# A transformer block's first stage on one Trainium2 core: its order of work rewritten, and four small products spread over the array

## The chip, the core and the metric

The kernel runs on one core of one Trainium2 chip. The metric is the device time of one execution in microseconds (us), and the number given for a kernel is the median of its runs. The core's engines are named as in the profile: PE is TensorE's matrix work and PEld its weight loads, DVE is VectorE, ACT is ScalarE, POOL is GpSimd, and SP is the queue on which most transfers are issued. PSUM is the memory that PE writes, in eight banks of 128 x 512 floats, which the code calls ps[0] to ps[7].

## The reference, cut to what matters

Two transformer blocks are computed for 256 tokens of width 1024. Only the beginning of the first concerns the change: the conditioning vectors c and c_ctx give a shift and a scale for the tokens x and for the context ctx; both are normalised and modulated with them; the results, called hT (tokens) and hcT (context) when turned so that features lie on the partitions, are multiplied by w_in. Beside it, filters for a long convolution come out of a small network with two sines, and their spectrum out of a Fourier matrix.

```python
x = x + _pos_embed_2d(ROWS)
mod_x = split(silu(c) @ w_ada[l] + b_ada[l], 6); mod_c = split(silu(c_ctx) @ w_ada[l] + b_ada[l], 6)
def project(h, mod):
    p = _modulate(_rmsnorm(h, norm_mix_g[l]), mod[0], mod[1]) @ w_in[l]
    q, k, v, g, a_f, a_b, hy = split(p, PROJ_SPLITS)
    la_f = log_sigmoid(a_f @ gla_wa_f[l] + gla_ba_f[l]) / 16      # la_b in the same way
hdn = sin(freq * (z @ w1 + b1)); hdn = sin(freq * (hdn @ w2 + b2))
h = (hdn @ w3).reshape(L, 2, 2, 512) * exp(-t * deltas)           # the filters
```

After this come gated linear attention, the long convolution, a mixture of experts, and a second pair of attention and feed-forward layers. The change leaves these as they are.

## The kernel before

Each engine runs its own list of instructions, written out by hand in one order; counters (semaphores) let one engine wait for another. There is no scheduler: an instruction that waits holds up all that stand behind it on its engine. Weights come in tiles of 128 rows through a ring of 12 slots, in the order of `load_order`; a slot is loaded again when `tiles_done`, which PE raises, says that its last user is through.

The first stage ends where the products for q, k and v begin (L1849 to L1851, three products of split operands each). On PE the functions of this stage are:

- `ada(m, k0, k1)` (L1787): conditioning row m = 0 (shift) or 1 (scale), 128 x 32 weights in four column groups at once, four weight tiles at a time.
- `mod(i, m)` (L1796): turns a finished row into columns, eight products of two columns. ACT copies the row out of PSUM before (`row`, L761) and the columns after it (`mod`, L767); four small POOL operations (L665 to L668) then make the factors a_mix and b_mix.
- `turn(src, ready)` (L1775): turns the normalised tokens xn or the context cn, 16 transposes; ACT copies the result to hT or hcT (`taken`, L754).
- `taps(o)` (L1812): four products of the filter network's last layer, for filter order o. DVE makes the filters of it (`filters`, L1207 to L1210).
- `spectrum(o)` (L1821 to L1823): ten products with the Fourier matrix. ACT copies the five results to spec (L775 to L779) and raises `ft_taken`.
- the loop over k = 0 to 7 that follows: per tile of w_in two wide products for the gate g (L1870, 512 columns each, weights hT) and two narrow ones (L1873, 32 x 256), of hT and of hcT, for the input of the decay gates. Before the change, `spectrum(1)` stands in the middle of this loop.

The products for q, k and v wait for `ft_taken` 2, since they write the banks that spectrum(1) used, and for `lo_ready` 1: the first tile of w_in must have been split in two parts, by ACT (`split_in`, L816) and then DVE (`low_in`, L1245). On ACT, `split_in(0)` stands behind the five copies of spectrum(1). This stretch of ACT's list is the same before and after the change:

```python
act.copy(hT_parts[0], hT[:, :, :]).then_inc(hcT_ready, 1)
act.wait_ge(hcT_ready, KD)
act.copy(hcT_parts[0], hcT).then_inc(hcT_ready, 1)
spectrum(1)
...
for i in range(PARTS_1):
    split_in(i)
```

Behind the products for q, k and v, four products with only 33 rows (L1901) give the decay gates' arguments; ACT and DVE take their logarithm, which the cumulative sums need after the first eight tiles of the hyena products (the next L1849 to L1851).

## Time and profile before

| | us |
|---|---|
| runs of the kernel before | 1566.29, 1573.41, 1570.35; median 1570.35 |
| the profiled execution | 1564.88, of which the span from its first to its last instruction is 1563.0 |
| PE busy in the span | 1317.6 (84%) |
| DVE, ACT busy | 639.7, 498.4 |
| first product for q, k and v starts at | 92.47 |

All places in the trace are microseconds from the start of the span of this one execution, and durations too are those of this execution. It took 5.47 us less than the median of the runs. Records of fp32 products come in pairs, so that eight records of L1812 are four products; a record's duration includes its way through the array, and back to back they follow each other sooner than they last.

### The profile page before, as it was taken

The page shows a single profiled execution, that of the slowest core. Times are in us where ns is not written, and L with a number is a line of the kernel's source. Part 1 is how long each engine was busy: PE and PEld are TensorE (multiplying, and loading weights), DVE is VectorE, ACT ScalarE, POOL GpSimd, SP SyncE. Part 2 cuts the span into 40 slices and gives each one's busy share as a digit, 9 for nine tenths or more (in the row PEclk, how much of TensorE's full clock was granted, in tenths as well). Part 3 has the DMA queues.
Part 4 walks back from the last instruction along what each step waited for, and adds up shares of the span by engine and source line. Part 5 has one row for each costly group of instructions (what it writes and reads, how often), then busy time and mean ns, then how long its engine had stood idle before and what let it go on. Part 6 is the DMA issues. An engine that isn't in the chain of part 4 may idle for free.

```text
span 1563.0 us, 22568 instructions
## 1 busy us (share of the span) xinstructions
PE 1317.6 (84%) x9346; PEld 968.9 (62%) x9346; DVE 639.7 (41%) x913; ACT 498.4 (32%) x757; POOL 103.1 (7%) x115
## 2 busy tenths in 40 slices
PE   5999899976655565655689999999999999999998
PEld 1468665731111111101186999999999987999997
DVE  4324545430100100100187575556545447565654
ACT  2423532320000000000157544345343437444443
POOL 0000011000000000000017000000000007000000
PEclk9999999888886967887799999999999999999999
DMA  9433536969999999999952356655666751355562
GB/s 354 156 108 83 161 135 242 413 275 416 420 419 419 420 419 419 420 419 419 384 186 63 109 174 196 189 167 162 194 190 184 205 171 55 97 165 172 178 205 74
DMA packets 136870, 376.55 MB, mean 241 GB/s; under 512 B 8392, under 2 KB 55929, under 8 KB 136608
## 3 DMA queue, kind: packets, MB, share of 16 engines
q1 hardware_dynamic: 134952, 373.81, 66.1%
q10 hardware_dynamic: 1848, 1.74, 0.3%
q8 instruction: 52, 0.85, 0.2%
q14 instruction: 18, 0.15, 0.0%
HBM read 373.42 MB, written 1.05 MB: 240 GB/s over the span
## 4 chain that ended last, share of the span: by engine, by line
PE 62%; DMA 20%; DVE 9%; ACT 4%; SPq 3%; issue 1%; POOL 1%; DVEq 0%; ACTq 0%
PE psum L1849 14%; PE psum L1851 14%; PE psum L1850 14%; DMA ring<-in_w_up 6%; DMA ring<-in_w_down 6%; DMA work<-in_w_gate 5%; PE psum L2139 4%; SPq L542 3%; DMA tokens<-in_w_down 1%; DVE parts L1496 1%; DVE route L1527 1%; POOL work L719 1%; PE psum L1870 1%; PE psum L2236 1%; PE psum L2011 1%
## 5 line engine op out<-in xcount | busy, mean ns | idle before, releaser
L1849 PE MATMUL psum<-parts 128*128 128x256 f32 (+1 forms) x1672 | 496.0, 297 | 12.9 <-DVE parts L1502 9.2
L1850 PE MATMUL psum<-parts 128*128 128x256 f32 (+1 forms) x1672 | 493.7, 295 | 0.0
L1851 PE MATMUL psum<-parts 128*128 128x256 f32 (+1 forms) x1672 | 493.4, 295 | 0.0
L1496 DVE TENSOR_TENSOR parts<-ring,parts 128x1024 fp32r<-128x1024 f32 x232 | 280.8, 1227 | 168.4 <-ACT parts L988 167.7
L1849 PEld LDWEIGHTS psum<-parts 128*128 128x128 f32 x1672 | 321.0, 192 | 24.4 <-issue 13.5
L1850 PEld LDWEIGHTS psum<-parts 128*128 128x128 f32 x1672 | 321.1, 192 | 7.3 <-issue 0.2
L1851 PEld LDWEIGHTS psum<-parts 128*128 128x128 f32 x1672 | 321.0, 192 | 7.3
L988 ACT CAST parts<-ring 128x1024 fp32r<-128x1024 f32 x232 | 239.8, 1045 | 248.2 <-PE psum L1851 211.5
L2139 PE MATMUL psum<-ring,work 128*32 128x512 f32 x512 | 87.8, 823 | 64.8 <-DMA ring<-in_w_up 34.3
L978 ACT ACTIVATE work<-psum 128x1024 f32<-128x1024 f32 x4 | 4.1, 1023 | 381.9 <-PE psum L2139 381.9
L2139 PE MATMUL psum<-work 128*32 128x512 f32 x512 | 83.8, 796 | 48.5 <-DMA work<-in_w_gate 29.3
L1479 DVE TENSOR_TENSOR work<-work,psum 128x1024 f32<-128x1024 f32 x4 | 4.9, 1220 | 271.1 <-ACT work L978 271.1
L2139 PEld LDWEIGHTS psum<-ring,work 128*32 128x32 f32 x512 | 16.6, 132 | 136.8 <-DMA ring<-in_w_up 52.5
L719 POOL TENSOR_SCALAR work<-work 128x256 f32<-128x256 f32 (+1 forms) x64 | 71.0, 1112 | 436.0 <-DVE work L1592 432.7
L2139 PE MATMUL psum<-early,work 128*32 128x512 f32 x384 | 56.6, 722 | 37.5 <-DMA early<-in_w_down 20.1
L2139 PEld LDWEIGHTS psum<-work 128*32 128x32 f32 x512 | 16.9, 130 | 111.3 <-DMA work<-in_w_gate 44.6
L1484 DVE SCALAR_TENSOR_TENSOR work<-psum,work,gate_ffn 128x512 f32<-128x512 f32 x8 | 5.6, 746 | 148.9 <-PE psum L2139 148.9
L2139 PEld LDWEIGHTS psum<-early,work 128*32 128x32 f32 x384 | 11.6, 121 | 79.7 <-DMA early<-in_w_down 29.8
L1079 ACT ACTIVATE work<-tokens 128x512 f32<-128x512 f32 x22 | 13.9, 632 | 104.0 <-DVE tokens L1626 104.0
L1849 PE MATMUL psum<-work_parts,ring_parts 128*128 128x256 f32 x144 | 42.3, 294 | 2.5 <-DVE ring_parts L1245 2.4
L1245 DVE TENSOR_TENSOR ring_parts<-ring,ring_parts 128x1024 fp32r<-128x1024 f32 (+1 forms) x24 | 25.0, 1046 | 47.1 <-ACT ring_parts L816 47.0
L1048 ACT ACTIVATE work<-work 128x257 f32<-128x257 f32 (+1 forms) x64 | 35.5, 557 | 23.6 <-DVE work L1592 23.5
(341 smaller groups left out, 1444.5 us busy)
## 6 DMA issues: line engine op xcount, KB each, us to landing
ring<-in_w_qkv_b SPq DMA_DIRECT2D x72, 512.0 KB, 4.3
work<-in_w_gate SPq DMA_DIRECT2D x16, 2048.0 KB, 23.0
ring<-in_w_up SPq DMA_DIRECT2D x16, 2048.0 KB, 23.4
ring<-in_w_ada SPq DMA_DIRECT2D x48, 512.0 KB, 8.2
work<-in_w_down SPq DMA_DIRECT2D x12, 2048.0 KB, 23.1
ring<-in_w_gate SPq DMA_DIRECT2D x44, 512.0 KB, 4.0
ring<-in_w_up SPq DMA_DIRECT2D x44, 512.0 KB, 5.4
ring<-in_w_down SPq DMA_DIRECT2D x44, 512.0 KB, 4.3
```

What stands on the lines that cost most here:

```text
L542: sp.dma_start(out, d[name][0, bass.ds(expert, EG), P * k:P * k + P, :].rearrange("j p n -> p j n")).then_inc(full, 16)
L719: ins = pool.tensor_scalar(bias_d[:, n % 2, j, 0:SPAN[layer]], dist[:, p], SLOPE[2 * k + j], None, ALU.mult)
L988: act.copy(part_of(hi_slots, t, n), ring[:, slot_2(t), 0:n]).then_inc(hi_ready, 1)
L1048: ins = act.activation(row, row, ACT.Exp, scale=-1.0, bias=nmax[:, p, h:h + 1], accum_out=den[:, p, h:h + 1])
L1245: dve.tensor_tensor(lower, w, high, ALU.subtract).then_inc(lo_ready, 1)
L1496: dve.tensor_tensor(part_of(lo_slots, t, n), ring[:, slot_2(t), 0:n], part_of(hi_slots, t, n), ALU.subtract).then_inc(lo_ready, 1)
L1527: return dve.tensor_reduce(sq_sum[:, L * i:L * i + L], sq.rearrange("p k l -> p l k"), AX.X, ALU.add)
L1849: pe.matmul(out, lhsT[0], rhs[0], start=start, stop=False, skip_group_check=True)
L1850: pe.matmul(out, lhsT[0], rhs[1], start=False, stop=False, skip_group_check=True)
L1851: return pe.matmul(out, lhsT[1], rhs[0], start=False, stop=stop, skip_group_check=True)
L1870: pe.matmul(ps[5 + t], hT[:, k, P * t:P * t + P], w[:, 0:V_W], start=(k == 0), stop=(k == KD - 1))
L2139: ins = pe.matmul(ps[bank + n][rows, :], lhsT[:, k, rows], w[:, j, 512 * n:512 * n + 512], start=(k == 0), stop=(k == KD - 1))
```

## The change

The conditioning products move between the parts of the filter network, the tokens are normalised and turned earlier and the context later, and the context is turned into the same banks 0 to 3 that the tokens used. The gate products wait for hT tile by tile (`hT_ready` counts to 8 for its eight parts, so later counts rise by 7 or 1). The narrow products leave the loop, follow the eight pairs of wide ones, and write partitions 0 to 31 and 64 to 95 of bank 7, in two column groups. The gates' input and its weights wa are laid out twice, at partitions 0 and 64, and the four products alternate between the two groups of rows. spectrum(1) comes last. The diff, cut to its core (the rest renumbers counters and lays out wa and aT for 97 partitions, which makes the transfer of wa 97 x 512 floats in place of 33 x 512, and splits DVE's copy to aT in two of 32 x 256):

```diff
-            sp.dma_start(decay, d["c_decay"].rearrange("p (a t h) -> p a t h", a=2, t=TT)).then_inc(filter_loaded, 16)
             sp.dma_start(consts[:, :], d["c_ident"]).then_inc(x_loaded, 16)
-            sp.dma_start(cn, d["ctx"][0].rearrange("(t p) d -> p t d", p=P)).then_inc(ctx_loaded, 16)
-            sp.dma_start(dft, d["c_dft"].rearrange("p (t f) -> p t f", t=TT)).then_inc(filter_loaded, 16)
             for t in load_order:
                 src, n = stream[t]
+                if t == upto_tile["ada0"]:
+                    sp.dma_start(decay, d["c_decay"].rearrange("p (a t h) -> p a t h", a=2, t=TT)).then_inc(filter_loaded, 16)
+                    sp.dma_start(dft, d["c_dft"].rearrange("p (t f) -> p t f", t=TT)).then_inc(filter_loaded, 16)
+                if t == upto_tile["ada1"]:
+                    sp.dma_start(cn, d["ctx"][0].rearrange("(t p) d -> p t d", p=P)).then_inc(ctx_loaded, 16)
...
-            for i in range(2):
+            def sine(i):
                 act.wait_ge(sin_arg, i + 1)
                 act.activation(hid[:, 2], hid[:, 0], ACT.Sin).then_inc(sin_done, 1)
 
+            def token_norm(i, x, out):
+                for t in range(TT):
+                    ins = act.activation(out[:, t], x[:, t], ACT.Square, accum_out=stats[:, 2 * i + t:2 * i + t + 1])
+                ins.then_inc(squared, 1)
+
+            def token_root(i):
+                act.wait_ge(ms_ready, i + 1)
+                act.activation(stats[:, 8 + 2 * i:10 + 2 * i], stats[:, 4 + 2 * i:6 + 2 * i], ACT.Sqrt).then_inc(std_ready, 1)
+
+            sine(0)
             act.wait_ge(x_placed, 1)
-            for t in range(TT):
-                act.activation(xn[:, t], xres[:, t], ACT.Square, accum_out=stats[:, t:t + 1])
-            act.wait_ge(ctx_loaded, 16)
-            for t in range(TT):
-                ins = act.activation(sq[:, t], cn[:, t], ACT.Square, accum_out=stats[:, 2 + t:3 + t])
-            ins.then_inc(squared, 1)
-            act.wait_ge(ms_ready, 1)
-            act.activation(stats[:, 8:12], stats[:, 4:8], ACT.Sqrt).then_inc(std_ready, 1)
+            token_norm(0, xres, xn)
+            sine(1)
+            token_root(0)
...
+            taken(1, hT)
             row(0)
+            mod(0)
             spectrum(0)
-            mod(0)
             row(1)
-            taken(1, hT)
             mod(1)
+            act.wait_ge(ctx_loaded, 16)
+            token_norm(1, cn, sq)
+            token_root(1)
...
+                if i == 0:
+                    dve.wait_ge(x_loaded, 48)
+                    dve.tensor_tensor(xres[:, :, :], xres[:, :, :], pos, ALU.add).then_inc(x_placed, 1)
+
+            def token_norm(i, x, out):
+                dve.wait_ge(squared, i + 1)
+                dve.tensor_scalar(stats[:, 4 + 2 * i:6 + 2 * i], stats[:, 2 * i:2 * i + 2], 1.0 / D, EPS, ALU.mult, ALU.add).then_inc(ms_ready, 1)
+                dve.wait_ge(std_ready, i + 1)
+                link(dve.reciprocal(stats[:, 12 + 2 * i:14 + 2 * i], stats[:, 8 + 2 * i:10 + 2 * i]))
+                for t in range(TT):
+                    at = 12 + 2 * i + t
+                    ins = dve.tensor_scalar(out[:, t], x[:, t], stats[:, at:at + 1], None, ALU.mult)
+                ins.then_inc(xn_ready, 1)
+
+            token_norm(0, xres, xn)
...
+                dve.tensor_scalar(hT[:, k, :], hT[:, k, :], a_mix[:, k, 0:1], b_mix[:, k, 0:1], ALU.mult, ALU.add).then_inc(hT_ready, 1)
+            token_norm(1, cn, cn)
...
+            ada(0, 0, 4)
+            pe.wait_ge(xn_ready, 1)
+            turn(xn, xt_ready)
+            ada(0, 4, 8)
+            pe.wait_ge(xt_taken, 1)
             taps(0)
-            ada(0, 0, 4)
+            mod(0, 0)
+            ada(1, 0, 4)
             pe.wait_ge(filter_loaded, 32)
             spectrum(0)
-            ada(0, 4, 8)
-            ada(1, 0, 8)
-            mod(0, 0)
-            pe.wait_ge(xn_ready, 1)
-            pe.wait_ge(ft_taken, 1)
-            turn(xn, xt_ready)
+            ada(1, 4, 8)
             mod(1, 1)
-            pe.wait_ge(xn_ready, 2)
-            pe.wait_ge(mod_taken, 2)
-            turn(cn, xt_ready, 4)
-            pe.wait_ge(xt_taken, 1)
-            taps(1)
 
             def products(out, lhsT, rhs, start, stop):
                 pe.matmul(out, lhsT[0], rhs[0], start=start, stop=False, skip_group_check=True)
                 return w_parts[i % PARTS_1]
 
 
-            pe.wait_ge(hT_ready, 1)
-            pe.wait_ge(xt_taken, 2)
+            ws = []
             for k in range(KD):
-                if k == 4:
-                    spectrum(1)
-                w = tile()
+                ws.append(tile())
+                pe.wait_ge(hT_ready, k + 1)
                 for t in range(TT):
-                    pe.matmul(ps[5 + t], hT[:, k, P * t:P * t + P], w[:, 0:V_W], start=(k == 0), stop=(k == KD - 1))
+                    pe.matmul(ps[5 + t], hT[:, k, P * t:P * t + P], ws[k][:, 0:V_W], start=(k == 0), stop=(k == KD - 1))
+                if k == 3:
+                    pe.wait_ge(xn_ready, 2)
+                    pe.wait_ge(ft_taken, 1)
+                    turn(cn, xt_ready)
+                if k == 5:
+                    pe.wait_ge(xt_taken, 2)
+                    taps(1)
+            for k, w in enumerate(ws):
                 pe.wait_ge(hcT_ready, k + 1)
                 for s, h in enumerate((hT, hcT)):
-                    ins = pe.matmul(ps[7][0:2 * RANK, L * s:L * s + L], w[:, V_W:V_W + 2 * RANK], h[:, k, :],
-                                    start=(k == 0 and s == 0), stop=(k == KD - 1), skip_group_check=True)
+                    ins = pe.matmul(ps[7][HID * s:HID * s + 2 * RANK, 0:L], w[:, V_W:V_W + 2 * RANK], h[:, k, :],
+                                    start=(k == 0), stop=(k == KD - 1), skip_group_check=True)
                 ins.then_inc(tiles_done, 1)
+            spectrum(1)
...
-            for i, b in enumerate((7, 0, 1, 2)):
+            for i, (b, s, t) in enumerate(((7, 0, 0), (1, 1, 0), (0, 0, 1), (2, 1, 1))):
                 if i == 1:
                     pe.wait_ge(q_taken, 1)
-                pe.matmul(ps[b], aT[:, P * i:P * i + P], wa, start=True, stop=True).then_inc(gatein_ready, 1)
+                rows = slice(HID * s, HID * s + 2 * RANK + 1)
+                pe.matmul(ps[b], aT[rows, P * t:P * t + P], wa[rows], start=True, stop=True).then_inc(gatein_ready, 1)
 
```

PE's list in the opening, with what each first instruction waits for. Before the change (L1812 taps, L1787 ada, L1821 spectrum, L1796 mod, L1775 turn, L1870 the first gate product; "ring_full" counts a weight tile's landing, and the rows left out are the further products of the same call):

```order
L1812 MATMUL psum<-work 128x512 [waits sin_done]
...
L1787 MATMUL psum<-ring,gate_ffn 32x512 [waits ring_full2,ring_full1,ring_full3,ring_full0,cond_ready]
...
L1821 MATMUL psum<-work,early 128x512 [waits filt_ready,filter_loaded]
...
L1787 MATMUL psum<-ring,gate_ffn 32x512 [waits ring_full6,ring_full7,ring_full5,ring_full4]
...
L1787 MATMUL psum<-ring,gate_ffn 32x512 [waits ring_full10,ring_full9,ring_full11,ring_full8,row_taken]
...
L1787 MATMUL psum<-ring,gate_ffn 32x512 [waits ring_full2,ring_full3,ring_full1,ring_full0]
...
L1796 MATMUL psum<-consts,early 128x2 [waits row_taken]
...
L1775 MATMUL psum<-consts,tokens 128x128 [waits ft_taken,xn_ready]
...
L1796 MATMUL psum<-consts,early 128x2 [waits mod_taken,row_taken]
...
L1775 MATMUL psum<-consts,work 128x128 [waits mod_taken,xn_ready]
...
L1812 MATMUL psum<-work 128x512 [waits xt_taken]
...
L1870 MATMUL psum<-ring,tokens 128x512 [waits ring_full4,xt_taken,hT_ready]
```

After it, in the lines of the changed kernel (L1801 ada, L1789 turn, L1826 taps, L1810 mod, L1835 spectrum, L1878 the gate products):

```order
L1801 MATMUL psum<-ring,gate_ffn 32x512 [waits ring_full1,ring_full2,ring_full0,ring_full3,cond_ready,sin_done]
...
L1789 MATMUL psum<-consts,tokens 128x128 [waits xn_ready]
...
L1801 MATMUL psum<-ring,gate_ffn 32x512 [waits ring_full6,ring_full7,ring_full5,ring_full4]
...
L1826 MATMUL psum<-work 128x512 [waits xt_taken]
...
L1810 MATMUL psum<-consts,early 128x2 [waits row_taken]
...
L1801 MATMUL psum<-ring,gate_ffn 32x512 [waits ring_full10,ring_full9,ring_full11,ring_full8,row_taken]
...
L1835 MATMUL psum<-work,early 128x512 [waits filt_ready,filter_loaded]
...
L1801 MATMUL psum<-ring,gate_ffn 32x512 [waits ring_full2,ring_full3,ring_full1,ring_full0]
...
L1810 MATMUL psum<-consts,early 128x2 [waits mod_taken,row_taken]
...
L1878 MATMUL psum<-ring,tokens 128x512 [waits hT_ready,ring_full4]
```

The first ada and the turning of xn stand ahead of the taps, and the second mod stands directly ahead of the gate products; the turning of cn and the second taps have left the opening.

PE's list at the end of the stage, before the change (L1870 wide, L1873 narrow, L1849 the first product for q, k and v):

```order
L1873 MATMUL psum<-tokens,ring 32x256 [waits hcT_ready]
...
L1870 MATMUL psum<-ring,tokens 128x512 [waits ring_full10]
...
L1873 MATMUL psum<-tokens,ring 32x256 [waits hcT_ready]
L1873 MATMUL psum<-work,ring 32x256
L1870 MATMUL psum<-ring,tokens 128x512 [waits ring_full11]
L1870 MATMUL psum<-ring,tokens 128x512
L1873 MATMUL psum<-tokens,ring 32x256 [waits hcT_ready]
L1873 MATMUL psum<-work,ring 32x256
L1849 MATMUL psum<-work_parts,ring_parts 128x256 [waits lo_ready,hT_ready,ft_taken]
```

and after it (L1878 wide, L1889 narrow, L1835 to L1837 the second spectrum, L1859 the first product for q, k and v):

```order
L1878 MATMUL psum<-ring,tokens 128x512 [waits hT_ready,ring_full10]
...
L1878 MATMUL psum<-ring,tokens 128x512 [waits hT_ready,ring_full11]
...
L1889 MATMUL psum<-tokens,ring 32x256 [waits hcT_ready]
L1889 MATMUL psum<-work,ring 32x256
...
L1889 MATMUL psum<-tokens,ring 32x256 [waits hcT_ready]
L1889 MATMUL psum<-work,ring 32x256
L1835 MATMUL psum<-work,early 128x512 [waits filt_ready]
...
L1836 MATMUL psum<-work,early 128x512
L1837 MATMUL psum<-work,early 1x512
L1859 MATMUL psum<-work_parts,ring_parts 128x256 [waits lo_ready,hT_ready,ft_taken]
```

The spectrum stood ten products of the gate loop ahead of the q, k and v products' wait for `ft_taken` and `lo_ready`; now it stands immediately ahead of it.

SP's list of transfers after the change, in its first part (L530 is the identity, L540 weight tiles, L534 and L535 the decay and Fourier tables, L537 the context):

```order
L530 DMA consts<-in_c_ident 128x130
L540 DMA ring<-in_w_ada 128x1024 x8
L534 DMA work<-in_c_decay 128x2048
L535 DMA early<-in_c_dft 128x1024
L540 DMA ring<-in_w_ada 128x1024 x4
L540 DMA ring<-in_w_ada 128x1024 [waits tiles_done] x4
L537 DMA work<-in_ctx 128x2x1024
L540 DMA ring<-in_w_in 128x544 [waits tiles_done] x8
```

Before, decay, context and Fourier tables, 2.5 MB together, were issued ahead of the first weight tile.

## Rows read from the trace of the kernel before

**Rows 1.** The page, the chain that ended last, by engine.
```profile
PE 62%; DMA 20%; DVE 9%; ACT 4%; SPq 3%; issue 1%; POOL 1%; DVEq 0%; ACTq 0%
```

**Rows 2.** Timeline of PE, opening: start us, us, work, idle before.
```profile
17.19 7.19 PE L1812 MATMUL psum<-work 64*128 64x512 f32 x8 [3.39 <-ACT work L738]
24.43 3.64 PE L1787 MATMUL psum<-ring,gate_ffn 128*32 128x512 f32 x16
29.49 2.05 PE L1821 MATMUL psum<-work,early 128*128 128x512 f32 x2 [1.42 <-DVE work L1210]
...
43.11 3.64 PE L1787 MATMUL psum<-ring,gate_ffn 128*32 128x512 f32 x32 [1.15 <-ACT early L761]
46.68 1.95 PE L1796 MATMUL psum<-consts,early 128*128 128x2 f32 x16
48.49 1.95 PE L1775 MATMUL psum<-consts,tokens 128*128 128x128 f32 x16
...
52.62 3.21 PE L1775 MATMUL psum<-consts,work 128*128 128x128 f32 x16 [0.50 <-ACT early L767]
55.76 4.05 PE L1812 MATMUL psum<-work 64*128 64x512 f32 x8
```

**Rows 3.** Timeline of PE, the gate products to the first split product.
```profile
60.18 1.95 PE L1870 MATMUL psum<-ring,tokens 128*128 128x512 f32 x4 [0.37 <-issue]
...
63.05 1.98 PE L1870 MATMUL psum<-ring,tokens 128*128 128x512 f32 x4
...
71.73 1.13 PE L1821 MATMUL psum<-work,early 128*128 128x512 f32 x2
...
92.47 0.39 PE L1849 MATMUL psum<-work_parts,ring_parts 128*128 128x256 f32 x1
```

**Rows 4.** Chain that ended last, one piece inside the second spectrum.
```profile
74.58 0.86 PE psum L1822 x2
```

**Rows 5.** Timeline of DVE, the same stretches.
```profile
16.61 2.28 DVE L1198 TENSOR_TENSOR xres<-xres,work 128x2048 f32<-128x2048 f32 x1
...
29.91 1.42 DVE L1218 TENSOR_SCALAR tokens<-xres,stats 128x1024 f32<-128x1024 f32 x2
...
53.74 2.67 DVE L1228 TENSOR_SCALAR tokens<-tokens,a_mix,b_mix 128x256 f32<-128x256 f32 x8 [21.09 <-POOL b_mix L668]
...
85.04 2.36 DVE L1245 TENSOR_TENSOR ring_parts<-ring,ring_parts 128x1024 fp32r<-128x1024 f32 x2 [14.51 <-ACT ring_parts L816]
```

**Rows 6.** Timeline of ACT, the same stretches.
```profile
23.20 1.28 ACT L748 ACT_TABLE_LOAD   x1
...
50.47 1.93 ACT L754 COPY tokens<-psum 128x1024 f32<-128x1024 f32 x2 [0.72 <-PE psum L1775]
...
81.00 0.58 ACT L775 COPY early<-psum 128x512 f32<-128x512 f32 x1 [13.19 <-PE psum L1823]
...
83.97 1.99 ACT L816 CAST ring_parts<-ring 128x1024 fp32r<-128x1024 f32 x2
```

**Rows 7.** Timeline of SP, the issue of the position table.
```profile
3.86 0.47 SPq L529 DMA_DIRECT2D work<-in_c_pos  x1
```

**Rows 8.** DMA issues up to 100 us: KB each, us to landing.
```profile
work<-in_c_pos SPq DMA_DIRECT2D x1, 1024.0 KB, 9.0
```

**Rows 9.** Windows; last three columns: granted clock, DMA share, GB/s.
```profile
15.00:20.00 5.00, 2.81 (x4) 1.25 (x5) 3.75 (x6) 1.50 (x4) 0.00 (x0) 1.00 1.03 420
50.00:55.00 5.00, 4.50 (x34) 4.44 (x33) 1.26 (x4) 2.00 (x3) 0.91 (x4) 0.81 0.99 374
130.00:140.00 10.00, 8.57 (x23) 4.21 (x22) 7.66 (x8) 4.07 (x6) 3.51 (x1) 0.75 0.19 58
140.00:150.00 10.00, 10.00 (x79) 10.00 (x79) 6.19 (x9) 6.80 (x5) 0.00 (x0) 0.91 0.22 54
```

**Rows 10.** Timeline of PE around the gate input and hyena products.
```profile
133.71 4.23 PE L1901 MATMUL psum<-early 33*128 33x512 f32 x6 [0.60 <-ACT early L828]
...
138.77 0.55 PE L1849 MATMUL psum<-work_parts,ring_parts 128*128 128x256 f32 x1 [0.83 <-DVE ring_parts L1245]
```

69 lines of the change are left out of this document (29 added, 40 removed).

## The prediction

> **What bounds the kernel now.** I read the page first. PE holds 62% of the chain that ended last and transfers 20% [rows 1], but the mean says little about the first stage, so I went to the timelines of its engines. From the first taps at 17.19 to the first product for q, k and v at 92.47, PE is the engine in front: the list below has waits of only 1.42, 1.15, 0.50 and 0.37 us [rows 2, 3]. The stage takes 75.3 us, and its end starts a long dense run of products. So what counts is the time at which that first product starts, and whatever delays it should delay the rest: the stages behind it wait for their predecessors' results, the expert weights' transfers too.
>
> Two more things are to be seen. The first taps take 7.19 us and the second, the same eight records, 4.05; 32 records of ada take 3.64 us at 43.11 and 16 take as long at 24.43 [rows 2]. So PE runs at its lower level, 1.2 GHz, from the start until the first spectrum. It falls there again near 53 us: the granted clock of 50 to 55 is 0.81 [rows 9], and the second turning takes 3.21 us where the first took 1.95 [rows 2]. Before that fall PE had two-column products, transposes and a wait.
>
> **The opening, step by step, on the changed order.** Adding the position table (2.28 us, [rows 5]) now stands between the two sines. The table lands at 3.86 + 9.0 = 12.9 [rows 7, 8], the identity, issued next, about 0.2 later (estimate from its 65 KB at 420 GB/s, [rows 9]), so the sum ends at 15.4. The second sine's chain took the 3.39 us of idle time before the taps [rows 2]; now it ends at 18.8, 1.6 later than before. The first four weight tiles landed by 24.43, since ada found them there [rows 2]. With 2.5 MB fewer ahead of them, at 420 GB/s, they land by 18.4 at the latest: no wait. The tiles of the second half, 2.1 MB behind, come by 23.4.
>
> - ada(0), first half: 18.8 to 22.4, the 3.64 us of the lower level.
> - The root for xn: table load 1.28 and scaling 1.42 [rows 5, 6], and some 0.4 of small operations (estimate), so xn is there at 21.9, under that ada.
> - Turning xn takes 1.95 us at the upper and 3.21 at the lower level [rows 2]. I take 2.3, to 24.7. ACT copies it in 1.93 [rows 6], to 26.6; ada's second half (half of 3.64, so 1.8) fits beneath.
> - taps 4.05, to 30.7. DVE's filters follow: taps ended at 24.38 before and the spectrum began at 29.49, 5.1 us [rows 2], so the spectrum can begin at 35.8. mod (1.81, from 46.68 to 48.49) and ada(1), first half (1.8), end at 34.4 beneath it, unless the clock falls again; I allow 0.7 for that.
> - spectrum: 71.73 to the copy at 81.00, 9.3 us [rows 3, 6], to 45.8.
> - ACT must now copy the spectrum (81.00 to 83.97, 3.0 us [rows 6]) before row(1), whose copy is the 1.15 us that PE waited at 43.11 [rows 2]. ada(1)'s second half hides under that, the rest is a new wait of 2.3 us. mod(1) then runs from 49.9 to 51.7, or 52.2 with 0.5 for a lower clock.
> - From the end of mod(1) to the first gate product lie ACT's copy, POOL's four operations and one of DVE's eight: PE's mod ended at 50.27 + 1.84 = 52.1, DVE began at 53.74 [rows 5], and its first eighth takes 0.3. That is 2.0 us, under which the old order had turned cn. It is now open. Gate products start at 54.2, against 60.18 [rows 3].
>
> **The gate products and the end.** Two records of full products take 0.86 us [rows 4], so a tile's four wide records take 1.72. A tile took 63.05 - 60.18 = 2.87 with its narrow ones [rows 3]: 1.72, 0.86 for the narrow four at half the width, and 0.3 for going to and fro between the shapes. After the change: eight times 1.72 is 13.8; the turning of cn is 1.9 and the second taps 4.3 with their switch, both taken from the opening. The context's normalisation, eight hT parts (2.67, [rows 5]) and the copies beside them have 6.9 us of wide products before they are wanted, and the second filters (5.1) have two wide pairs and the narrow products (7.2). So these cost nothing; if any came 1 us late, PE would wait that 1 us.
>
> The narrow products in two column groups: no row has two groups. Ada has four, with a record every 3.64 / 32 = 0.114 us [rows 2], so 32 narrow records would take 3.6, against 6.9 one after another. I take 3.6 plus 0.2. From 54.2: 13.8 + 1.9 + 4.3 + 3.8 brings 78.0. PE has stood in small products and waits from 47.6 to 54.2, so I expect the clock to fall, as it did near 53. At the other place where PE stood and had small products, from 132 on, the windows 130 to 150 lose 0.25 x 10 + 0.09 x 10 = 3.4 us of clock [rows 9], of which about half fell on working PE; the fall near 53 cost 1.3. I take 2.1, bounds 1.3 and 3.4: 80.1. The spectrum brings 89.4.
>
> Here is the change's price. Before, the copies of spectrum(1), and the split of the first tile behind them on ACT and DVE, ran under four tiles of gate products. Now nothing lies between. From 81.00 through the splitting casts at 83.97 and DVE's first half of 2.36, begun at 85.04 [rows 5, 6], is 5.2 us, all of it open: 94.6. The clock falls during it, 1.9 more: 96.5. Against 92.47 that is **+4.0 us**.
>
> **The gate input** in two row groups. It occupied PE from 133.71 to 137.94, but the hyena products began at 138.77, released by DVE's split of their first tile [rows 10]. Its saving, at most half of 4.23, is thus hidden; if DVE were faster by over 0.8, it would show. I count zero, and -2.1 as the bound. DVE's copy to aT in two pieces and the longer transfer of wa lie under q, k and v: zero, at most 0.3.
>
> Own time: 1564.88 + 4.0 = 1568.9. The median of the runs was 5.47 above that execution, so the predicted median is 1570.35 + 4.0, rounded 1574.5 us.
>
> **The rivals.** *The clock stays low through the opening.* In the trace PE was at work for 7.19 and then 3.64 us and stayed at 1.2 GHz [rows 2]. If the same holds with ada and the turning in front, then turning ends at 25.6, ada at 29.3, the taps' 7.2 at 36.5, mod and ada (double) at 43.8, the spectrum, partly low, at 54.8. That is 9 later than 45.8: +13, 1583, slower by over 0.5%. It decides as soon as the lower level lasts to about 35 us. Against it: at 53 to 57 a turning of 3.21 was followed by quick taps, so a dense stretch of transposes did bring the clock back. The Trainium skill (TensorE: Matmul & The Clock Gate, part 1) has the clock rise with sustained activity; by it the old taps should have raised it, and they did not, while the new mix would raise it and give the sum above. I give this rival 0.14.
>
> *Column groups do not overlap.* Then 3.3 us are added: +7.3, 1577.7. For it: no row has two groups at partitions 0 and 64. Against it: ada's four overlap fully. The Trainium skill (TensorEngine Tiling, Key Properties) says that tiles load and multiply in parallel, which would be the 3.6. Chance 0.07.
>
> *The delay is given back or the gains are larger.* The opening delivers gate products 6 us earlier, and if the wait at the end cost nothing, because ACT's copies or the split ran beneath something, the sum would be 4.0 - 5.2 - 1.9 = -3: 1567. Together with the gate input's 2.1 it is 1565; past 0.5% it comes only with another few us that I cannot place. Against it: ACT's list keeps the split behind the copies. Chance 0.19, of which 0.06 lies below 1562.5.
>
> **How the numbers follow.** My forecast, 0.60, has its own range: with every clock loss at its lower bound and turning at 1.95 the sum is +1, with all at the upper and ada's second half low it is +8: 1571 to 1578.5. The range for 8 in 10 reaches to both sides, from the small gain to near the low clock's case: 1566 to 1582. About 0.5%, 7.9 us, is what a measurement here can tell from no change. Slower by more: the low clock's 0.14, half of the column groups', 0.05 of the forecast: 0.22. Faster by more: 0.06, rounded 0.07. Within: 0.71.
>
> **What would show it.** Right: gate products begin near 54; narrow records come every 0.11; PE idles some 5 us after the second spectrum, with a granted clock below 1 there; the first q, k, v product starts at 94 to 98; the gate input shortens and hyena products still wait for DVE. Wrong: taps of 7 us again; an idle time at the end under 2 us; q, k, v below 91; or a difference of more than 2 us that arises behind the hyena products.

## The result and the profile after

| | before | after |
|---|---|---|
| median of 20 runs each, us | 1568.27 (1560.51 to 1574.57) | 1574.24 (1571.37 to 1577.34) |
| ratio after to before | | 1.0041, 95% interval 1.0029 to 1.0053 |
| profiled execution, us (span) | 1564.88 (1563.0) | 1576.28 (1574.4) |

The changed kernel is slower by 0.41%, 6.4 us (4.5 to 8.3). That is clear of no difference at all, and for the most part inside the 0.5% that the prediction took as no change. The forecast was +4.0 on the median that was shown, 1574.5; the kernel before came 2.1 us lower in these runs, so the forecast of the time is met to 0.3 us and that of the difference missed by 2.4. The closeness of the first is luck. The two profiled executions differ by 11.4 us, because that of before lies 3.4 us below its median and that of after 2.0 above: not the spans are to be compared but places inside them.

First PE's timeline of the changed kernel, from the first product of ada to the first product of q, k, v (start us, us, work, idle time before in brackets with its releaser); it answers to [rows 2, 3].

```profile
18.63 3.64 PE L1801 MATMUL psum<-ring,gate_ffn 128*32 128x512 f32 x16 [4.73 <-ACT work L740]
25.24 1.92 PE L1801 MATMUL psum<-ring,gate_ffn 128*32 128x512 f32 x16
27.32 3.70 PE L1826 MATMUL psum<-work 64*128 64x512 f32 x8 [0.16 <-ACT tokens L760]
36.14 1.10 PE L1835 MATMUL psum<-work,early 128*128 128x512 f32 x2 [1.39 <-DVE work L1233]
49.39 1.95 PE L1810 MATMUL psum<-consts,early 128*128 128x2 f32 x16 [2.34 <-ACT early L767]
53.37 9.76 PE L1878 MATMUL psum<-ring,tokens 128*128 128x512 f32 x16 [2.03 <-DVE tokens L1240]
62.97 1.91 PE L1789 MATMUL psum<-consts,work 128*128 128x128 f32 x16
64.71 3.60 PE L1878 MATMUL psum<-ring,tokens 128*128 128x512 f32 x8
69.91 4.80 PE L1826 MATMUL psum<-work 64*128 64x512 f32 x8 [1.60 <-ACT work L760]
74.64 5.95 PE L1878 MATMUL psum<-ring,tokens 128*128 128x512 f32 x8
80.52 0.40 PE L1889 MATMUL psum<-tokens,ring 128*32 128x256 f32 x1
80.76 0.38 PE L1889 MATMUL psum<-tokens,ring 128*32 128x256 f32 x1
84.10 1.12 PE L1835 MATMUL psum<-work,early 128*128 128x512 f32 x2
98.77 0.55 PE L1859 MATMUL psum<-work_parts,ring_parts 128*128 128x256 f32 x1 [5.45 <-DVE ring_parts L1257]
```

Gate products begin at 53.37, 6.8 us sooner than at 60.18 [rows 3]; the first product of q, k, v begins at 98.77, 6.3 later than at 92.47. So the stretch between these two rows has grown by 13 us. Some 5.4 of them are no loss: the context's turning (1.74 to the next row) and the second taps (3.6 at the upper level) stood in the opening before. And the narrow products in column groups save about as much again. The waits and the slow stretches thus cost some 13 us. Four things are to be seen in the list: a wait of 5.45 at the end, as forecast; one of 1.60 ahead of the second taps, which was not; and two stretches in which the same records take longer: 16 wide ones 9.76 and eight 5.95, where eight take 3.60 between them. The taps between them are slower too, 4.80.

The windows of the changed kernel say why (granted clock, DMA share and GB/s are the last three columns):

```profile
50.00:55.00 5.00, 2.97 (x14) 2.09 (x15) 2.19 (x7) 2.25 (x5) 0.91 (x4) 0.69 0.80 329
55.00:60.00 5.00, 5.00 (x9) 2.01 (x8) 2.15 (x6) 0.20 (x1) 0.00 (x0) 0.63 0.46 154
70.00:75.00 5.00, 5.00 (x9) 1.83 (x10) 0.19 (x1) 4.25 (x9) 0.00 (x0) 0.74 0.03 6
95.00:100.00 5.00, 1.23 (x6) 1.26 (x7) 2.60 (x3) 4.97 (x7) 0.00 (x0) 0.63 0.00 2
```

Each fall to the lower level stands behind small products or a wait: mod and its waits ahead of 53, the 1.60 ahead of 70, the 5.45 ahead of 99. The third has to be read with care. The prediction put its price ahead of the first product of q, k, v, but the loss lies behind the row 98.77. From the first product for q, k, v to the first hyena product it took 46.30 us before and takes 48.25 now, 1.95 more. The products for q, k and v are the same, and what the gate input behind them saved on PE was waited for again (below). So the start of the hyena products is the better place at which to compare the two kernels. PE's timeline there, in the changed kernel, answers to [rows 10]:

```profile
141.96 1.98 PE L1919 MATMUL psum<-early 33*128 33x512 f32 x6 [0.60 <-ACT early L837]
147.02 0.55 PE L1859 MATMUL psum<-work_parts,ring_parts 128*128 128x256 f32 x1 [3.08 <-DVE ring_parts L1257]
```

147.02 - 138.77 = +8.25 us, as much as the whole loss by the ratio and more. Behind this place the two profiled executions differ by another 3.15 us (11.4 in all); against the kernel before, the other kernels' traces differ there by between -2.4 and +2.8, so I read nothing into it. The gate input's six records shrank from 4.23 to 1.98, and PE's wait for DVE in front of the hyena products grew from 0.83 to 3.08 by the same 2.25: no gain.

Not all of the 2.25 is the row groups' doing. The run e6 below has this part as it was, four products on one group of rows, and there (PE's timeline, and a window):

```profile
130.08 2.84 PE L1903 MATMUL psum<-early 33*128 33x512 f32 x6 [0.60 <-ACT early L828]
130.00:133.00 3.00, 2.84 (x6) 1.04 (x6) 3.00 (x3) 0.57 (x3) 3.00 (x1) 1.00 0.38 152
```

The granted clock is 1.00 there, and was 0.79 from 133.7 to 136 and 0.50 from 136 to 138 in the kernel before. So 0.86 us are the row groups' (2.84 to 1.98, both at the upper level), and 1.39 the place of the clock's fall.

The wait of 1.60 has its cause on ACT. Its timeline (ACTq is its instruction queue, which issues DMAs):

```profile
57.10 0.31 ACTq L800 DMA_DIRECT2D early<-in_wa  x1
59.83 7.58 ACTq L804 DMA_DIRECT2D route<-in_c_iota  x1
67.93 1.93 ACT L760 COPY work<-psum 128x1024 f32<-128x1024 f32 x2 [12.13 <-issue]
93.36 0.58 ACT L781 COPY early<-psum 128x512 f32<-128x512 f32 x1 [14.92 <-PE psum L1837]
96.33 1.99 ACT L825 CAST ring_parts<-ring 128x1024 fp32r<-128x1024 f32 x2
```

The turned context was in PSUM by 64.9, but ACT copied it at 67.93 because an issue held its list for 7.58 us. In the kernel before, the same issue:

```profile
55.46 2.17 ACTq L795 DMA_DIRECT2D route<-in_c_iota  x1
```

Until about 63 other transfers share the engines, and from then to the end of the issue nearly nothing else moves. Three windows of the changed kernel, and then its group of wa in the view of DMA issues (KB each):

```profile
60.00:62.00 2.00, 2.00 (x6) 0.91 (x5) 0.00 (x0) 0.00 (x0) 0.00 (x0) 1.00 0.99 341
64.00:66.00 2.00, 2.00 (x12) 1.29 (x10) 0.00 (x0) 0.00 (x0) 0.00 (x0) 1.00 0.07 26
66.00:68.00 2.00, 2.00 (x6) 0.76 (x4) 0.00 (x0) 0.07 (x1) 0.00 (x0) 1.00 0.07 26
```

```profile
early<-in_wa ACTq DMA_DIRECT2D x1, 194.0 KB
```

A DMA share of 0.07 is one of the 16 engines (0.0625), and the issue ended at 67.41, when that lone traffic did: the share of 66 to 67.4 is 0.06 and that of 67.4 to 69 is 0.41. My reading was that wa, whose 33 rows became 97, goes through a single engine, and that an issue behind it waits until this has drained. 194 KB at 26 GB/s take 7.6 us, like the stall, but the transfer was issued at 57.10, 10.3 us before the stall's end, and other traffic was on the engines for much of that, so that this match proves nothing. What exactly the issue waits for (room in a queue, I supposed) no run shows.

### The profile page after: what moved, and what is told of

Read it like the earlier page. It is cut to its first block, busy times and chain, and to the rows that moved or that the text cites. A ratio compares the mean times of both kernels' runs of the same rounds, so it can differ in the third digit from the quotient of the medians.

```text
span 1574.4 us, 22580 instructions
## 1 busy us (share of the span) xinstructions
PE 1317.1 (84%) x9346; PEld 975.3 (62%) x9346; DVE 640.2 (41%) x917; ACT 499.0 (32%) x758; POOL 103.2 (7%) x115
## 4 chain that ended last, share of the span: by engine, by line
PE 61%; DMA 18%; DVE 9%; ACT 5%; SPq 4%; issue 1%; POOL 1%; ACTq 1%; DVEq 0%
PE psum L1859 14%; PE psum L1860 14%; PE psum L1861 14%; DMA ring<-in_w_up 6%; DMA ring<-in_w_down 6%; DMA work<-in_w_gate 5%; PE psum L2157 5%; SPq L544 4%; DVE parts L1510 1%; DVE route L1541 1%; PE psum L2029 1%; PE psum L2254 1%; POOL work L721 1%; PE psum L2022 1%; PE psum L2277 1%
## 5 line engine op out<-in xcount | busy, mean ns | idle before, releaser
L1859 PE MATMUL psum<-parts 128*128 128x256 f32 (+1 forms) x1672 | 496.7, 297 | 12.9 <-DVE parts L1516 9.2
L1859 PEld LDWEIGHTS psum<-parts 128*128 128x128 f32 x1672 | 321.7, 192 | 24.4 <-issue 13.8
L2157 PE MATMUL psum<-ring,work 128*32 128x512 f32 x512 | 82.3, 777 | 72.0 <-DMA ring<-in_w_up 36.3
L2157 PE MATMUL psum<-work 128*32 128x512 f32 x512 | 86.0, 815 | 42.8 <-DMA work<-in_w_gate 24.6
L1859 PE MATMUL psum<-work_parts,ring_parts 128*128 128x256 f32 x144 | 43.2, 300 | 10.2 <-DVE ring_parts L1257 10.1
```

The source lines that it names most:

```text
L1859: pe.matmul(out, lhsT[0], rhs[0], start=start, stop=False, skip_group_check=True)
L2157: ins = pe.matmul(ps[bank + n][rows, :], lhsT[:, k, rows], w[:, j, 512 * n:512 * n + 512], start=(k == 0), stop=(k == KD - 1))
```

## The experiments

The theory: the loss has three parts, the open wait behind the second spectrum with its clock loss, the stall of wa with the clock loss that follows from it, and the loss in the opening, against gains from the column groups. The rivals are named run by run. All edits are to the changed kernel, except that of e6. "Hyena" is the start of the hyena products against 138.77 in the kernel before.

| kernel | executions | ratio to before | 95% | in us | q, k, v at | hyena |
|---|---|---|---|---|---|---|
| the change | 20 | 1.0041 | 1.0029 to 1.0053 | +6.4 | 98.77 | +8.3 |
| e1 spectrum ahead of narrow | 10 | 1.0010 | 0.9988 to 1.0032 | +1.6 | 93.91 | +3.0 |
| e2 split ahead of copies | 10 | 1.0010 | 0.9988 to 1.0031 | +1.6 | 95.93 | +6.2 |
| e3 issues late | 8 | 1.0034 | 1.0017 to 1.0052 | +5.3 | 98.97 | +8.7 |
| e4 wait filled | 10 | 1.0023 | 1.0010 to 1.0036 | +3.6 | 97.83 | +6.9 |
| e5 wa on 128 rows | 10 | 1.0018 | 1.0004 to 1.0033 | +2.8 | 93.21 | +2.8 |
| e6 columns only | 7 | 0.9967 | 0.9946 to 0.9989 | -5.2 | 88.79 | -3.6 |
| e7 row first | 4 | 1.0059 | 1.0038 to 1.0079 | +9.2 | 100.40 | +9.4 |
| e8 combined | 10 | 0.9969 | 0.9954 to 0.9984 | -4.9 | 87.50 | -5.0 |
| e9 wa on 98 rows | 1 | | | | 94.04 | +4.2 |
| e10 wa on 106 rows | 1 | | | | 92.54 | +2.7 |

The last column comes from one trace each, and the ratios' intervals are some 4 to 7 us wide; still the two agree within 5 us everywhere, and within 1 in three of the nine that have both. The intervals of e1 to e5 and e7 overlap that of the change, some only at the edge. So for the single edits the mechanism is read from the traces, and only e6 and e8 are told from the change by their times alone. A trace's places scatter too: from the first q, k, v product to the first hyena product the six traces with the same end wait of 5.45 took 47.8 to 48.9 us.

**e1, the second spectrum ahead of the narrow products.**

```diff
+            spectrum(1)
             for k, w in enumerate(ws):
                 pe.wait_ge(hcT_ready, k + 1)
...
-            spectrum(1)
```

> The changed kernel with its second spectrum put ahead of the eight narrow pairs instead of behind them. Theory (the exposed end chain: after the spectrum come ACT's copies, 3.0 us, and the split of the first tile, 2.4 us, with PE idle for 5.45): the narrow products, 3.6 us, now lie over the copies, the wait before the first q, k, v product falls from 5.45 to about 1.6, while up to 1.5 us appear ahead of the spectrum, whose filters are ready only at 79.7 in the changed kernel's trace: that product starts 2 to 3.5 us earlier (98.8 becomes 95.3 to 96.8), and the kernel takes 2 to 5 us less, ratio to the changed kernel 0.997 to 0.999. Rival (the delay comes from the opening and from the context, and the engines behind give the end's wait back): the wait shrinks but the time of the kernel stays.

PE's timeline of this run:

```profile
70.51 3.70 PE L1826 MATMUL psum<-work 64*128 64x512 f32 x8 [1.19 <-ACT work L760]
79.23 1.12 PE L1835 MATMUL psum<-work,early 128*128 128x512 f32 x2 [1.39 <-DVE work L1233]
93.91 0.36 PE L1859 MATMUL psum<-work_parts,ring_parts 128*128 128x256 f32 x1 [2.00 <-DVE ring_parts L1257]
```

Of the wait, 3.45 us came back under the narrow products; a wait of 1.39 opened ahead of the spectrum, whose filters had lost their cover. The place of the end wait is shown, and the edit is worth 2.1 us at the first q, k, v product. That product came 4.9 us sooner, beyond the 2 to 3.5 expected. The rest is not the edit's: the taps of this trace and the eight wide records behind them ran at the upper level (3.70 each, against 4.80 and 5.95).

**e2, ACT splits the first two tiles ahead of the spectrum's copies.**

```diff
             act.copy(hcT_parts[0], hcT).then_inc(hcT_ready, 1)
-            spectrum(1)
...
             for i in range(PARTS_1):
                 split_in(i)
+            spectrum(1)
```

> The changed kernel with ACT splitting the first two weight tiles ahead of its copies of the second spectrum. Theory (exposed end chain): only the copies remain behind the spectrum, so PE's wait falls from 5.45 to about 3.1 and the first q, k, v product starts at about 96.4; the kernel takes 2 us less. Rival (PE waits for the copies alone, and the split was never last): the wait stays at 5.4.

```profile
95.93 0.58 PE L1859 MATMUL psum<-work_parts,ring_parts 128*128 128x256 f32 x1 [3.15 <-ACT early L785]
```

PE now waits for ACT's last copy out of PSUM, not for the split: the wait is made of the copies (3.0 us) and the split behind them. The order of ACT's list is worth 2.3 us of the wait, and the copies are the floor.

**e3, the nine issues behind the context's copy.**

```diff
+            taken(2, hcT)
             act.dma_start(brow, d["b_ada"]).then_inc(gla_loaded, 16)
...
             act.dma_start(spread, d["c_spread"]).then_inc(route_loaded, 16)
-            taken(2, hcT)
```

> The changed kernel with ACT's nine transfer issues behind the copy of the context instead of ahead of it. In the changed kernel's trace these took from 55.6 to 67.9, one of them 7.58 us, and the copy that the second taps need ran behind them; PE idled 1.60 us and its clock then fell for 6.8 us. Theory (the issues hold up the context): the wait of 1.6 before the second taps goes, the clock stays up there, taps and the last wide pairs take 4.1 and 3.5 instead of 4.8 and 6.0, and the first q, k, v product starts 4 to 5 us earlier, at about 94.3; kernel 4 us less. Rival (the clock fell because taps fill only half the rows, whatever the wait): the wait goes, but the taps and wide pairs still take over 9 us together, and only 1.6 us are won.

ACT's queue, and then PE, in this run:

```profile
70.49 7.19 ACTq L805 DMA_DIRECT2D route<-in_c_iota  x1
```

```profile
72.94 3.70 PE L1878 MATMUL psum<-ring,tokens 128*128 128x512 f32 x8
78.92 0.40 PE L1889 MATMUL psum<-tokens,ring 128*32 128x256 f32 x1 [2.28 <-ACT work L810]
98.97 0.55 PE L1859 MATMUL psum<-work_parts,ring_parts 128*128 128x256 f32 x1 [5.45 <-DVE ring_parts L1257]
```

A miss, and a useful one. The wait ahead of the taps is gone and their clock loss with it, as expected. But the stall stayed as long and now stood ahead of ACT's scaling of the context, so PE waited 2.28 us there, and q, k, v began at 98.97 instead of near 94.3. A blocked list is not cured by moving what blocks it behind one consumer when the next one stands right behind.

**e4, products that nobody reads in the end wait.** 15 of them go to an unused part of a bank; the result is not touched.

```diff
             spectrum(1)
+            for i in range(5):
+                for j in range(1, 4):
+                    pe.matmul(ps[4][32 * j:32 * j + 32, :], ident[:, 0:32], dft[:, 0], start=True, stop=True, skip_group_check=True)
```

> The changed kernel with fifteen additional products, in three column groups of bank 4 that nobody reads, between the second spectrum and the first q, k, v product. They take about 4.4 us of the 5.45 that PE idles there and change no wait. Theory (the idle time also costs the clock): the granted clock stays at 1 there, the q, k, v products start at the same 98.8 but at full pace, and the stage behind ends some 2 us earlier (in the changed kernel PE ran its first 4.4 us of them at half pace); kernel 2 us less. Rival (the clock has no part, or the additional products delay the first real one): no gain, or 0 to 1 us later.

Windows of this run; the changed kernel has 0.53 and 0.61 in the same ones.

```profile
96.00:100.00 4.00, 2.17 (x14) 2.21 (x15) 3.10 (x4) 3.68 (x4) 0.14 (x1) 0.85 0.00 0
100.00:104.00 4.00, 4.00 (x17) 3.42 (x17) 0.00 (x0) 0.00 (x0) 2.23 (x1) 0.72 0.00 0
```

The fall came later and was shorter, but it came: 1.97 us were still open. From q, k, v to hyena the trace took 47.83 us, 0.42 less than the change and no less than e7 with its whole wait (47.79). The 2 us expected did not come, and a gain of the filling is not shown. That the clock costs something there is shown otherwise: this stretch takes 46.3 us in the kernel before, in e6 and in e8, whose waits ahead of it are nil and 0.83, and 47.8 or more in all the others, whose waits are 2.0 or more.

**e5, wa on 128 rows.** The same data with zero rows below.

```diff
-        wa = cut(at, 2 * QK_W, parts=HID + 2 * RANK + 1); at += 512
+        wa = cut(at, 2 * QK_W); at += 512
...
-    wa = np.zeros((HID + 2 * RANK + 1, 2 * QK_W), np.float32)
+    wa = np.zeros((P, 2 * QK_W), np.float32)
```

> The changed kernel with the gates' weights wa laid out and loaded for 128 partitions instead of 97. In the changed kernel's trace ACT's issues after that transfer were held up, one for 7.58 us, and the traffic fell to some 26 GB/s from 64 to 68 us, as if one of the 16 DMA engines carried all 97 rows; before the change wa had 33 rows and the same issue took 2.17. Theory (97 rows go to one engine and ACT's list stands still behind it): the longest issue falls to about 2 us, the context is copied by 67, PE's wait of 1.60 before the second taps and the low clock behind it go (taps and last wide pairs 3.7 and 3.7 instead of 4.8 and 6.0), the first q, k, v product starts about 4 us earlier, at 94 to 95.5. Rival (the issues wait because of the router's 1024 small rows, whatever wa's form): the issue stays at 7 us.

ACT of this run, and then PE:

```profile
59.62 0.60 ACTq L804 DMA_DIRECT2D route<-in_c_iota  x1
64.37 1.93 ACT L760 COPY work<-psum 128x1024 f32<-128x1024 f32 x2 [7.97 <-PE psum L1789]
```

```profile
71.32 3.70 PE L1878 MATMUL psum<-ring,tokens 128*128 128x512 f32 x8
78.53 1.13 PE L1835 MATMUL psum<-work,early 128*128 128x512 f32 x2
93.21 0.55 PE L1859 MATMUL psum<-work_parts,ring_parts 128*128 128x256 f32 x1 [5.45 <-DVE ring_parts L1257]
```

More bytes, and no stall: 0.60 instead of 7.58. The copy follows PE at once, the wait of 1.60 is gone, and with it the second fall of the clock (eight wide records 3.70 instead of 5.95). The end wait is the same 5.45. This one edit takes 5.4 us from the start of the hyena products; by the ratios it is some 3.6 us, with intervals that just overlap.

**e9 and e10, 98 and 106 rows.** Was it the count of rows or their bytes? The edits are those of e5 with 98 and 106 for P. Each ran once (1571.44 and 1569.39 us, beside 1563.23 for one execution of the kernel before), which is too little for a ratio: only their traces are used.

> The changed kernel with wa on 98 rows of 2 KB instead of 97, one zero row more. In the changed kernel the transfer of wa's 97 rows holds ACT's list: the issue of c_iota takes 7.58 us, and 26 GB/s move meanwhile at a DMA share of 0.07, one sixteenth; with 128 rows the issue took 0.60. Theory: the row count decides over how many of the 16 DMA engines the transfer spreads, by its divisors up to 16. 98 = 14 x 7 spreads over 14, so the issue of c_iota takes 0.6 to 1 us and the context's copy waits for PE's turning. By the Trainium skill (DMA: Bandwidth & Descriptors, Why a DMA increments its semaphore by 16 and not by 1) the largest divisor up to 16 of the slowest dimension is the number of engines used. Rival: any count that is not a multiple of 16 goes through one engine; then the issue takes 7.6 us as with 97. Second rival: the stall grows with the bytes; then it is 7.6 or a little more too. Start of the first q, k, v product: 93 to 94 by the theory, 98 to 99 by the rivals.

> The changed kernel with wa on 106 rows of 2 KB, 2 x 53, nine zero rows more than the 97. Theory (the largest divisor up to 16 sets the number of DMA engines): two engines carry 212 KB at twice the 26 GB/s seen, some 4.1 us, so the issue of c_iota takes 3 to 4.2 us, and the DMA share meanwhile is 0.12 to 0.14. Rival, all counts that are not multiples of 16 go through one engine: 8.3 us at a share of 0.07. Rival, the stall comes of something else than the number of engines (the bytes): 8 us or 0.6. The context's copy then starts near 64.4, when PE's turning is done, by the theory, and the first q, k, v product at 93 to 94.

The issue in the two runs, 98 rows first:

```profile
59.27 0.74 ACTq L804 DMA_DIRECT2D route<-in_c_iota  x1
```

```profile
57.80 4.69 ACTq L804 DMA_DIRECT2D route<-in_c_iota  x1
```

One row more than 97 takes the stall away; 106 rows, 2 x 53, leave 4.69 us of it. So neither the bytes nor "not a multiple of 16" decide, and the order 97, 106, 98, 128 (7.58, 4.69, 0.74, 0.60 us) is that of one, two, 14 and 16 engines. With 97 rows the stall lay between 6.37 (e4) and 7.69 (e7) over six traces, above the 4.69 in each. In both new runs the context's copy came directly behind PE's turning and the second taps had no wait. 4.69 is above the 3 to 4.2 expected, and the share was not 0.13 but 0.8 to 0.9 from 58 to 62, since other transfers were still on their way; so two engines are inferred from the order and not seen in the share. The Trainium skill (DMA: Bandwidth & Descriptors, Why a DMA increments its semaphore by 16 and not by 1) states this rule: the number of engines is the largest up to 16 that divides the slowest dimension on both sides of the transfer. These runs agree.

**e6, the kernel before with the narrow products in two column groups and nothing else.**

```diff
-                    ins = pe.matmul(ps[7][0:2 * RANK, L * s:L * s + L], w[:, V_W:V_W + 2 * RANK], h[:, k, :],
+                    ins = pe.matmul(ps[7][HID * s:HID * s + 2 * RANK, 0:L], w[:, V_W:V_W + 2 * RANK], h[:, k, :],
```

> The kernel before with one part of the change alone: the narrow products in two column groups, where they stand in the loop. Theory (this part is a gain by itself, lost under the new order's waits): two narrow products run in the time of one, 0.43 us less per tile, the gate loop is 3.4 us shorter, the first q, k, v product starts at about 89.1 instead of 92.5, and the kernel takes 3 us less than before, ratio 0.998. Rival (column groups do not overlap when the shapes alternate with full products): the loop's period stays at 2.87 us and the ratio at 1.

PE's timeline of this run:

```profile
62.34 1.98 PE L1872 MATMUL psum<-ring,tokens 128*128 128x512 f32 x4
64.81 1.98 PE L1872 MATMUL psum<-ring,tokens 128*128 128x512 f32 x4
```

DVE's copy to aT follows the two places. A tile's period is 2.47 us where it was 2.87 [rows 3]; eight tiles give 3.2, and q, k, v begin 3.7 sooner (0.3 of it stood ahead of the gate products already). The kernel is faster than before, 0.9967 (0.9946 to 0.9989).

**e7, ACT's row(1) and mod(1) ahead of the first spectrum's copies.**

```diff
             mod(0)
-            spectrum(0)
             row(1)
             mod(1)
+            spectrum(0)
```

> The changed kernel with ACT copying the second conditioning row and its columns ahead of the first spectrum's five copies instead of behind them. Theory (new wait in the opening behind those copies, PE idle 2.34 us): PE waits about 1.1 us there, the second mod and the first gate product start 1.2 to 1.8 us earlier (53.4 becomes 51.6 to 52.2); at the end of the stage this is 1 to 2 us. Rival (DVE or POOL need the spectrum's copies first): nothing moves.

```profile
47.79 2.29 PE L1810 MATMUL psum<-consts,early 128*128 128x2 f32 x16 [1.15 <-ACT early L767]
70.03 7.19 PE L1826 MATMUL psum<-work 64*128 64x512 f32 x8 [3.67 <-ACT work L760]
100.40 0.55 PE L1859 MATMUL psum<-work_parts,ring_parts 128*128 128x256 f32 x1 [5.45 <-DVE ring_parts L1257]
```

The opening gained as expected: gate products from 52.11. But ACT's issue of c_iota began at 59.83 as before and took 7.69, so the context's copy came at 68.05, no sooner. PE came to it earlier and waited 3.67 instead of 1.60, and the taps behind ran wholly at the lower level, 7.19. What was saved ahead of the stall was lost at it, and in this trace more: the hyena products began 1.2 us later than in the change, where 1 to 2 us less was expected. The times (four executions) do not tell it from the change.

**e8, three edits together.** wa on 128 rows (e5), row first (e7), and on PE the turning after the second tile, the taps after the fourth, the second spectrum after the seventh, so that a wide tile and the narrow products stand behind it.

```diff
-                if k == 3:
+                if k == 1:
                     pe.wait_ge(xn_ready, 2)
...
-                if k == 5:
+                if k == 3:
                     pe.wait_ge(xt_taken, 2)
                     taps(1)
+                if k == 6:
+                    spectrum(1)
...
-            spectrum(1)
```

> The changed kernel with the three mends together: wa on 128 partitions, the second row ahead of the first spectrum's copies, and the second spectrum no longer last (the context turned after gate tile 1, second taps after tile 3, second spectrum after tile 6, so that the last wide pair and the narrow products, 5.3 us, lie over the copies and the split, 5.2 us). Theory (the change lost by its exposed ends alone and its parts are gains): PE's wait before the first q, k, v product is under 1 us, that product starts at 86 to 89 instead of 98.8, and the kernel is 3 to 6 us faster than the kernel before, ratio 0.996 to 0.998. Rival (an earlier stage only meets later waits): the first product is early, but the ratio stays at 1.000 or above.

```profile
51.89 6.17 PE L1878 MATMUL psum<-ring,tokens 128*128 128x512 f32 x8 [2.03 <-DVE tokens L1240]
81.11 1.98 PE L1878 MATMUL psum<-ring,tokens 128*128 128x512 f32 x4
87.50 0.36 PE L1859 MATMUL psum<-work_parts,ring_parts 128*128 128x256 f32 x1 [0.83 <-DVE ring_parts L1257]
```

The end wait is 0.83 and the kernel faster than the one before, 0.9969 (0.9954 to 0.9984). That is no more than e6 reached with a fraction of the edits: the two intervals overlap nearly wholly, and these runs cannot tell which is the better.

## Why the prediction was right, and where a term of it was not

The direction and the mechanism at the end were right: the delay of the first q, k, v product through a wait that nothing covers. Step by step:

**The opening.** ada began at 18.63 (forecast 18.8), the first spectrum at 36.14 (35.8), mod(1) waited 2.34 (2.3), and gate products began at 53.37 (54.2). The rival of a clock that stays low through the opening is refuted by the durations: the second half of ada took 1.92 and the taps 3.70, the upper level's, where the kernel before had 7.19 for the taps at 17.19 [rows 2]. The rule of the Trainium skill (TensorE: Matmul & The Clock Gate, part 1) that sustained activity raises the clock, which I had set against that rival, agrees with the new order; it left unexplained why the old taps alone did not, and no run here shows why. One reading of the prediction needs a caution. The lower level in the opening is told from records of double length alone. The granted clock of the windows is 1.00 there, in the kernel before [rows 9, 15 to 20] and in the changed one, in whose window 20 to 25 the first ada still ran at half pace and the turning took 3.11 where it later took 1.91:

```profile
20.00:25.00 5.00, 5.00 (x27) 3.00 (x20) 1.58 (x3) 0.09 (x1) 0.00 (x0) 1.00 1.03 421
```

So in the first 25 us that column and the durations disagree, and which of them tells the clock there is open. In the windows from 50 us on they agree.

**The gate products.** The narrow records came every 0.11 and took 84.10 - 80.52 = 3.6 (forecast 3.8): the rival in which column groups don't overlap is refuted, by e6 too. The first fall of the clock cost 9.60 us for 16 wide records against twice 3.60, so 2.4 (forecast 2.1).

**The step that failed** is "the longer transfer of wa lie[s] under q,k,v: zero, at most 0.3", and with it that the context's chain has "6.9 us of wide products" of cover and costs nothing. From 54.2 to 80.1 were forecast, 25.9 us; from 53.37 to 84.10 it took 30.7. The 4.8 are the wait of 1.6, 1.0 us on the taps (4.73 until the next row, against 3.70), and 2.3 on the eight wide records (5.95 against 3.70 in e5). I had counted the bytes of the transfer and the time at which its data are wanted, and not what its issue does to those behind it. The trace of before had an issue of 2.17 us among others of 0.4, so that an issue could be seen to hold the list. It was no clear hint at the row count, though: 33 has the divisor 11, where 97 has none but 1 and 106 only 2, and from 55.5 to 57.6 the DMA share was 1.02 with 399 GB/s moving. "If any came 1 us late, PE would wait that 1 us" was too mild as well: the wait of 1.6 came with 3.3 us of lower clock on the work behind it. That this belongs to the wait is borne out by the runs, though not by every one: the five traces without a wait ahead of the taps (e3, e5, e8, e9, e10) have no second fall there, and of the five with one (1.2 to 3.7 us) four have it.

**The end.** Spectrum to copy 9.26 (forecast 9.3), the open chain 5.4 (5.2), the clock's loss 1.95 (1.9; in the six traces with this wait 1.5 to 2.6); this last was placed ahead of the first product for q, k, v and lies behind it. e1 shows what covers the wait, e2 what it is made of, and e8, where both the wait and the loss are nearly gone, that they go together; e4 could not part them.

**The sum.** Set against 96.5, the comparable time is 98.77 + 1.95 = 100.7. The difference of 4.2 is -0.8 in the opening, +4.8 in the gate products and +0.2 at the end. In e5, with the mis-sized term away, the hyena products start 2.8 us late, and the ratio gives 2.8 (0.6 to 5.2): 1.2 under the forecast's +4.0, nearly all of it between the first gate product and the spectrum (78.53 - 53.97 = 24.6 against 25.9: some 0.7 each on the first fall and on the taps, 0.2 each on turning and narrow products, less some 0.4 on the wide ones).

That the predicted time, 1574.5, stands 0.3 us from the measured 1574.24 is luck: the kernel before was taken 2.1 us too high and the difference 2.4 too low. By the prediction's own signs, 98.77 lies 0.8 outside its 94 to 98 for the first q, k, v product, and 3.15 us of the profiled pair's difference lie behind the start of the hyena products where over 2 was to count against it; the other traces scatter as widely there.

**The gate input** gave nothing, as forecast: 2.25 us less on PE, of which 0.86 by the row groups, and 2.25 more of waiting for DVE. The column groups, tried alone, gain 5 us by e6's ratio and 3.6 by its trace, and the re-ordering around them, as first written, costs more than that.

What stays open: whether e6 or e8 is the better kernel, why the second fall of the clock did not come in e1 behind a wait of 1.19, while it came in e4 behind one of 1.24, and what the blocked issue waits for.

## What to carry to other kernels

Before a transfer's shape is changed, look at the issues behind it on the same engine and at what that engine must do next; a count of rows with a large divisor up to 16 costs some zero rows and can free the list. When a step is moved to the end of a stage, sum up the chain behind it on every engine (here spectrum copies, split, add), because what had run under it is moved with it. Take a gain in isolation first: the part that gained was worth as much alone as with the re-ordering around it even when that had been mended (e6 and e8). And a shorter stretch of PE is not yet the new form's doing: look at its granted clock, and if possible at the old form at the same level.

## What was not expected of the hardware

- Behind the other traffic, from 63 us on, 97 rows of 2 KB moved at 26 GB/s with one of 16 engines at work, and an issue behind them held ACT's list for 7.58 us; 98, 106 and 128 rows gave 0.74, 4.69 and 0.60 us.
- A wait of PE of 1.6 us in the middle of the gate products was followed by a granted clock of 0.74 in the window 70 to 75, and eight wide records took 5.95 instead of 3.70 us: the work behind a wait lost more than the wait. Four of the five traces with a wait there show it, and e1 (1.19 us) does not.
- In the first 25 us the granted clock of the windows was 1.00 while PE's records took twice their later length.
